# One ScalarE reordering in a four-mixer decoder trunk: two low rank products and an attention output go ahead of three dense copies and a weight split

## The reference

```
h = RMSNorm_pre(x);  P = h @ W_in
y_A = HGRN2(P_A); y_B = DSA(P_B); y_C = RWKV7(P_C); y_D = FoX(P_D)
m = sum_n sigmoid(P_gate_n) * (y_n @ W_branch_n)
x = x + RMSNorm_post(m @ W_out)
x = x + RMSNorm_post(relu(RMSNorm_pre(x) @ W_up)^2 @ W_down)
```

```
w_log = -softplus(-(w0 + tanh(w_in) @ w2)) - 0.5
a     = sigmoid(a0 + a_in @ a2)
g     = sigmoid(g_in) @ g2
v     = v + (v_first - v) * sigmoid(v0 + (v @ v1) @ v2)
```

## Time and profile before

| | |
|---|---|
| median of 3 runs | 2124.2 us (2123.23 to 2169.52) |
| profiled execution: its own time, its span | 2117.45 us, 2115.6 us |
| busy share: PE, ACT, DVE, POOL | 94%, 38%, 44%, 48% |
| granted TensorE clock, mean | 0.977 |
| chain that ended last, largest parts | issue 52%, POOL `w_lo` `L1446` 21%, `L1476` 17% |

### The profile page before, as it was taken

The page is one execution under the profiler, slowest core; times in us unless marked ns, Lnnn a source line. Parts: engine busy times, 40 slices in busy tenths (PEclk is TensorE's granted clock), DMA queues, the critical chain, the costliest instruction groups (busy, mean ns, idle before and its releaser), DMA issues.

```text
span 2115.6 us, 33629 instructions
## 1 busy us (share of the span) xinstructions
PE 1994.5 (94%) x11692; PEld 1551.5 (73%) x11692; DVE 940.1 (44%) x1688; ACT 794.5 (38%) x1276; POOL 1007.3 (48%) x1231
## 2 busy tenths in 40 slices
PE   6999989999998999999889999999999989999995
PEld 5876756777686888888668767577776768888884
DVE  6737865323332513224277478653234324223143
ACT  6434355234334412222354343552344253222134
POOL 5444514314467446557544444142154665555574
PEclk9999999999999999999889999999999999999998
DMA  4122311002122222222212222111121222222232
GB/s 172 71 81 70 100 31 50 32 32 71 52 88 80 80 99 98 91 99 100 71 57 81 81 80 80 35 47 33 40 66 55 80 80 100 94 94 99 89 101 99
DMA packets 50362, 161.87 MB, mean 77 GB/s; under 512 B 5280, under 2 KB 13600, under 8 KB 49952
## 3 DMA queue, kind: packets, MB, share of 16 engines
q1 hardware_dynamic: 49056, 157.05, 22.3%
q10 hardware_dynamic: 1152, 2.86, 0.4%
HBM read 157.79 MB, written 2.10 MB: 76 GB/s over the span
## 4 chain that ended last, share of the span: by engine, by line
issue 52%; POOL 42%; PE 3%; POOLq 1%; DVE 1%; DMA 0%; ACT 0%; SPq 0%; DVEq 0%; ACTq 0%
POOL w_lo L1446 21%; POOL w_lo L1476 17%; POOL slab L1466 2%; PE bank L554 1%; PE bank L556 1%; PE bank L555 1%; POOL rstd L1455 1%; POOL slab L1487 1%; POOLq L1473 0%; POOL slab L1469 0%; DMA w_raw<-wproj 0%; POOLq L1442 0%; DVE u_lo L1545 0%; DVE u_hi L1556 0%; DVE u_lo L1557 0%
## 5 line engine op out<-in xcount | busy, mean ns | idle before, releaser
L1446 POOL TENSOR_TENSOR w_lo<-w_raw,w_hi 128x256 fp32r<-128x256 f32 x624 | 496.4, 827 | 760.0 <-ACT w_hi L1064 759.7
L554 PE MATMUL bank<-hn_hi,w_hi 128*128 128x512 f32 x1312 | 548.3, 418 | 18.8 <-DVE hn_lo L1545 17.3
L1476 POOL TENSOR_TENSOR w_lo<-w_raw,w_hi 128x256 fp32r<-128x256 f32 x512 | 382.8, 779 | 300.4 <-ACT w_hi L1406 300.4
L555 PE MATMUL bank<-hn_lo,w_hi 128*128 128x512 f32 x1312 | 515.8, 393 | 0.0
L556 PE MATMUL bank<-hn_hi,w_lo 128*128 128x512 f32 x1312 | 515.6, 393 | 0.0
L554 PEld LDWEIGHTS bank<-hn_hi,w_hi 128*128 128x128 f32 x1312 | 248.6, 189 | 97.8 <-issue 25.1
L554 PE MATMUL bank<-u_hi,w_hi 128*128 128x512 f32 x736 | 293.2, 398 | 24.0 <-POOL w_lo L1438 11.4
L1406 ACT ACTIVATE w_hi<-w_raw 128x1024 fp32r<-128x1024 f32 x128 | 135.8, 1061 | 439.3 <-DMA w_raw<-wrest 414.3
L555 PE MATMUL bank<-u_lo,w_hi 128*128 128x512 f32 x736 | 289.2, 393 | 0.0
L556 PE MATMUL bank<-u_hi,w_lo 128*128 128x512 f32 x736 | 288.8, 392 | 0.0
L556 PEld LDWEIGHTS bank<-hn_hi,w_lo 128*128 128x128 f32 x1312 | 248.5, 189 | 53.7
(11 more groups left out here) (316 smaller groups left out, 2551.0 us busy)
## 6 DMA issues: line engine op xcount, KB each, us to landing
w_raw<-wrest SPq DMA_DIRECT2D x144, 512.0 KB, 3.5
w_raw<-wmerge SPq DMA_DIRECT2D x80, 512.0 KB, 3.6
w_raw<-wproj SPq DMA_DIRECT2D x64, 512.0 KB, 3.6
x<-x_in SPq DMA_DIRECT2D x4, 512.0 KB, 7.1
slab<-rope ACTq DMA_DIRECT2D x2, 1024.0 KB, 4.9
out<-x SPq DMA_DIRECT2D x4, 512.0 KB, 2.6
con<-tables SPq DMA_DIRECT2D x1, 898.0 KB, 11.2
slab<-masks SPq DMA_DIRECT2D x1, 896.0 KB, 12.9
```

Source lines behind the costliest of these rows:

```text
L554: mm(o_, stat[0], mov[0], start=first, stop=False)
L555: mm(o_, stat[0], mov[1], start=False, stop=False)
L1446: ins = pool.tensor_tensor(wlo[:, s_, cs], wraw[:, s_, cs], whi[:, s_, cs].bitcast(f32), SUB)
L1476: ins = pool.tensor_tensor(wlo[:, s_, cs], wraw[:, s_, cs], whi[:, s_, cs].bitcast(f32), SUB)
```

## The change

ScalarE's four takings of the low rank products are divided. After the sigmoid `L1193`, and only for mixer B's attention, it waits for `c_mix` 4, takes products 0 and 1 and the last attention output, and only then calls `take_steps`, with the three dense copies and the weight split. Products 2 and 3 follow where all four stood. For mixer D's attention (`which` = 1) the order stays. No other engine's code is changed.

```diff
                     if which == 0:
                         fn(S(15, 0)[64:128, :], S(15, 0)[64:128, :], ACT.Sigmoid)
+                        act.wait_ge(*c_mix.at(L, 4))
+                        lora_taken(0, 4)
+                        lora_taken(1, 5)
+                        attn_out(which, NT - 1)
                     take_steps(REACH[("bd"[which] + "_att", 15, 1)])
-                    attn_out(which, NT - 1)
+                    if which:
+                        attn_out(which, NT - 1)
+
+                def lora_taken(i_, b):
+
+                    act.wait_ge(*c_lw.at(L, i_ + 1))
+                    t = i_ % FT
+                    fn(S(2 + i_ // FT, t), ps[b][:, :], ACT.Sigmoid, bias=pcol("w0" if i_ < FT else "a0", t)).then_inc(*c_sg.up())
...
                 attention(0, 0)
-                act.wait_ge(*c_mix.at(L, 4))
-
-                def lora_taken(i_, b):
-
-                    act.wait_ge(*c_lw.at(L, i_ + 1))
-                    t = i_ % FT
-                    fn(S(2 + i_ // FT, t), ps[b][:, :], ACT.Sigmoid, bias=pcol("w0" if i_ < FT else "a0", t)).then_inc(*c_sg.up())
-                for i_ in range(3):
-                    lora_taken(i_, 4 + i_)
+                lora_taken(2, 6)
                 lora_taken(3, 4)
```

## The result

| | before | after |
|---|---|---|
| median of the comparison | 2123.72 us | 2110.44 us |
| ratio, 95% interval | | 0.9944 [0.9927, 0.9961] |
| profiled execution: own time, span | 2117.45, 2115.6 us | 2109.9, 2108.1 us |
| granted clock, mean | 0.977 | 0.977 |

The medians differ by 13.3 us where 6.5 were forecast; the ratio of 0.9944 is 11.9 us, and in two later comparisons it was 0.9950 and 0.9951, some 10.5 us. Some executions of a kernel take 2144 us or more at a lower granted clock (one of the four of before here), and the ratios and the medians of the table of experiments leave them out.

What follows compares the result with a forecast made beforehand. TensorE was taken as the bound, busy nearly all the time, with a removable wait for ScalarE. 4.3 us of idle time plus 2.2 of clock made 6.5 us, from 2124.2 to 2117.7 us; own range 2112.5 to 2122.9.

Steps and rivals of the forecast that it cites:

- The stall and its removal: TensorE ahead of product 3: its 2.16 us wait for ScalarE to free bank 4 goes, 4.3 us over two layers.
- The rows that were to show it: Profile signs: `L702` wait gone or below 0.5 us, its last pair behind product 2, `L1305` 2 us earlier, `L848` about 3.1.
- so I take the middle, 2.2 us: TensorE's clock behind the idle time, both layers: gain from fewer falls taken as 2.2 us, between 0 and 4.4.
- The upper bound of 4.4: Clock falls from product 3 on: 1.4 and 3.0 us in the layers, against 6.1 us for the stretch at 2.4 GHz.
- The baseline: Whole kernel: the gain on the profiled 2117.45 us was taken as the same from the median shown, 2124.2 us.
- My range: Whole kernel: 2112.5 to 2122.9 us, with 3 us each way for clock falls elsewhere.
- The moved weight split: ScalarE's split for `gate1`, 5 ends 1.5 us later, GpSimd's low part near 313; over 10 us of cover, cost nothing.
- The overlap of VectorE and GpSimd: `L1838` and `L1839` beside GpSimd's delayed low part: 0 to 2.2 us of VectorE time, taken as 1.1, costed at 0.
- the cover of 1.84 us: VectorE's wait at `L1843` for ScalarE's `L1305`, 1.84 us, was to hide VectorE's smaller gain and its slowdown beside GpSimd.
- rival 2: VectorE beside GpSimd: both overlapped operations lose 1.08 us, up to 1.8 us per layer comes back; 2121.3 us, chance 7%.
- The idle time did not move to `L848`: Rival at `L848`: VectorE's chain or a weight's arrival sets its time, TensorE waits 3.1 + 2.16 us; 2124.2, chance 8%.
- the narrow work of 7 us in a row: Rival, 302.4 to 309.4: unbroken narrow matmuls bring a longer clock fall than idle time did; slower, 2125.5 us, chance 4%.

Runs made afterwards that it cites:

- before_filled: Kernel before, with 8 full-size matmuls of unused result put into TensorE's idle 2.16 us ahead of product 3: 2115.63 us, ratio 0.9967.
- output_first: Changed kernel with only the last attention output ahead of the dense copies, all four products behind them as before: 2124.39 us, ratio 1.0003.
- before_late_split: Kernel before, with only ScalarE's second weight split moved behind the reciprocal norm that VectorE's last chain ahead of `L848` waits for: 2117.39 us, ratio 0.9978.
- products_first: Changed kernel with only products 0 and 1 ahead of the dense copies, the attention output behind copies and split: 2110.70 us, ratio 0.9937.
- more_dense: Changed kernel with 4 more steps of dense work placed ahead of `L848` (17 instead of 13): 2121.66 us, ratio 1.0020.
- products_again: Repetition of the changed kernel with only products 0 and 1 ahead of the dense copies, attention output behind them: 2110.32 us, ratio 0.9952.

## Why the prediction was wrong

**The stall and its removal: right.** The rows that were to show it do: no wait of `L702`, products 2 and 3 back to back, `L1305` (now 1308) 4.0 us earlier against product 0, the wait at `L848` at 3.2 us. This term, 2 x 2.16 = 4.3 us, stands.

**The step that failed: "so I take the middle, 2.2 us" for the clock.** In the profiles the two stretches lost 4.03 and 5.63 us, 9.66 together; less the idle 4.32 the clock's part is 5.3 us. Filling the wait alone took 4.9 us off them. I was wrong twice. The upper bound of 4.4 used 6.1 us for the stretch at full clock, and it is 5.9 in before_filled: the four branch steps, priced at 3.16 us with a slow first one, take 2.96 there. And I let `L972` stand against the idle time as cause with equal weight. Products on four rows are not products on thirty-two: the stretch at 302.4, with the very same products and a clock of 1.00, was the nearer row and gave the right answer. Over all profiles, the five with the idle time (before twice, wait lengthened, output first, later split on before) show a fall there in ten of ten layers, and the nine with the idle time removed or filled in none of eighteen. By the table the first layer of before's two profiles, with 10.8 and 10.7 us, was a mild case: output_first and before_late_split took 12.3 to 12.8 in both layers.

**The baseline.** I carried a profiled execution's gain to the median of three runs, 2124.2, without a word on how the kernel's runs scatter. Runs of before in the next comparison read 2113.66 to 2126.08 us. The sum of the corrected terms, 4.32 + 5.34 = 9.66 us, is 2114.5 from that median: inside the range, and still 4 us above 2110.4. It agrees with the ratios of 0.9950 and 0.9951. My range allowed 3 us for falls elsewhere around a wrong centre.

**Hidden terms: right in the result, partly by luck.** The moved weight split cost nothing, GpSimd's low part ended at 313.1 and the wait at `L848` rose by about 0.1 us. The overlap of VectorE and GpSimd cost 0.4 us per operation of the pair, 0.8 in all where I took 1.1. But two small instructions beside them lost another 0.9 us (the copy at 308.60 took 0.53 us instead of 0.17, `L1843` 0.68 instead of 0.16), which I had not counted. Against product 0, `L1305` comes 4.0 us earlier, and VectorE is ready for it only 1.4 us earlier (at 314.60 instead of 316.96). So the cover of 1.84 us was overdrawn by 0.8, by the mechanism of my rival 2, and ScalarE's table loads, a cover that I had not named, took this in with 0.4 us to spare. The Trainium skill (SBUF — State Buffer, "Who interferes with whom") says that a VectorE instruction with two SBUF inputs contends with a GpSimd instruction that reads SBUF. The trace agrees: both sides got slower, GpSimd's four pieces from 3.69 to 5.06 us.

**The rivals.** None came as a time. The idle time did not move to `L848`; the narrow work of 7 us in a row brought no fall at all.

**Open:** why the clock falls less elsewhere in products_first than in the changed kernel, and why the part between the layers was short when the wait was lengthened. Both ask how falls elsewhere depend on a shift of the timeline, which these runs don't control.

## What to carry to other kernels

Read the granted clock behind each wait of TensorE before costing it: here a wait of 2.16 us cost about 4.8 us (9.66 over two layers), because the matmuls behind it ran at 1.2 GHz. Whoever cannot remove such a wait can fill it with full-size matmuls whose result nobody uses; that also tests whether the clock is part of the cost. Before moving dense filler work to an idle place, look at what it held up where it stood.

## What the runs showed of the hardware

A clock at 0.50 lasted 44 us while PE was busy for 10.00 of each 10 us, as the profile counts it, with narrow level products and dense 128x512 steps between them (windows of more_dense). The same code at 356 us in the first layer was as busy and had 1.00. So a busy engine alone does not bring the clock back. It is not this edit's alone: the profiled execution of output_first has such a stretch of 31 us in the second layer, and that of products_first (2162.78 us) three of 41 us each in the first, in mixer C too. The Trainium skill (TensorE: Matmul & The Clock Gate, Part 1) describes the clock as set by how busy TensorE has been; by the busy column of the profile that does not hold here.

VectorE and GpSimd slow each other by amounts that depend on who meets whom: the scan pair took 3.27 us beside GpSimd, 2.86 beside it in products_again and 2.59 nearly without it in the changed kernel. The `TENSOR_TENSOR` on 128x1024 took 1.23 us alone, 1.66 and 1.75 beside weight splits and 2.31 beside GpSimd's additions of 128x512.
